# One table set for logarithm and exponential, an earlier query norm, and adaLN column sums by 32x32 transposes in a two-layer hybrid block

## The chip, the cores and the metric

The kernel runs on one core of one Trainium2 chip. The metric is the device time of one execution in microseconds (us). Engines are named as in the profile: PE (matrix multiply, with PEld for its weight loads), DVE (vector), ACT (scalar, with function tables), POOL, and the queue SP that issues most transfers.

## The reference, cut to what matters

Two layers over 256 tokens of width 1024, fp32. Each layer is: feed-forward, token mixer, feed-forward. Each of the three is preceded by an RMS norm that is modulated by columns of `mod` (adaLN), and its result is added through a gate column of `mod`.

```
cond = silu(c)                                   # one vector of 1024
for l in range(2):
    mod = cond @ w_ada[l] + b_ada[l]             # 1024 x 9216, split in 9
    h = rms_norm(x, g0) * (1 + sc1) + sh1
    x = x + 0.5 * g1 * swiglu(h, w_ff_in[l,0], w_ff_out[l,0])
    h = rms_norm(x, g1) * (1 + sc2) + sh2
    x = x + g2 * token_mix(h, ...)
    h = rms_norm(x, g2) * (1 + sc3) + sh3
    x = x + 0.5 * g3 * swiglu(h, w_ff_in[l,1], w_ff_out[l,1])
```

`token_mix` projects h to three branches. Branch a is windowed attention with RMS-normed queries and keys (logarithm and exponential for the norm, exponential for the softmax). Branch b is a gated linear recurrence with a short convolution (tanh, exponential, a square root made of logarithm and exponential, gelu). Branch c is chunked linear attention with decays (exponential, output norm). Sigmoid gates are made of tanh.

## The kernel before

Activations lie transposed: features on the 128 partitions, 256 tokens along the free dimension, x in eight chunks. Every fp32 weight matrix is read in slabs of 1024 x 256 (or 256 x 1024), 120 per layer. ACT rounds a slab to its high part (`hi`, L890), DVE subtracts to get the low part (`lo`, L1306), and PE makes each product in three passes (high-high, high-low, low-high; L460), 48 matmuls per slab. The four raw buffers, three high and three low buffers go round in turn, guarded by counters.

There are five programs written out by hand, one per engine, which meet only at semaphores. So the order on each engine is the order in the text. A wait is told below by its semaphore.

**Feed-forward.** `ff` runs j over 11 blocks of hidden features. In one step PE does the next gate slab, the down slab and the next up slab; ACT does silu and two or three `hi`; DVE does the product `t512b` (L1388), its low part (L1392), and three `lo`.

**adaLN.** `mod` is made in blocks of 512 columns, 18 per layer. For a block, DVE multiplies eight 128 x 512 pieces of `w_ada` by the entries of cond and sums them in `ada_acc` (`weigh`, L1225 and L1231, two halves per block). That leaves sums over 128 partitions still to be made. PE makes them in `ada(b)` (L504): four matmuls with a 128 x 128 piece of `ada_acc` as weights and a column of ones as the moving operand, so that each gives 128 sums down one PSUM column. DVE copies the four columns to `mod` (L1240). A table spreads the halves over steps j (`FF_HALVES`). In the feed-forwards, 20 blocks are made: six in each of the first three and two in the last. Six of the 20 are late: their `ada(b)` stands in the norm that follows, between the sum of squares (L554) and the first product. The 14 others stand in the steps j. Other blocks are made in the prologue (4) and beside the mixer's last products (12, four of them late, in the norm before the second feed-forward).

**Norm.** PE sums squares (L554). ACT makes rstd by logarithm (L897) and exponential (L899). DVE makes the modulation columns `ms` and `ma` (L1314 to L1317) from `mod`, then `hf` chunk by chunk (L1332); ACT rounds (L916), DVE subtracts (L1337), and PE starts its next product by chunks as they come (`by_chunks`, L485, or the key/value product, L605).

**Function tables.** ACT holds one set of functions at a time. Where the program asks for a function that isn't in the set that is loaded, the compiler puts an ACT_TABLE_LOAD in front of it. Before, the logarithm comes from one set and the exponential (with tanh) from another; gelu with tanh and silu with tanh come from two more; copy, square, identity and abs are in every set.

**Mixer, first part.** Four rounds i. Each has four slabs: queries (p), recurrence input (p+1), gelu gate (p+2), branch c gate (p+3). The softmax and the recurrence of round i-1 are done inside round i. In the order of each engine, round i has:

- PE: product p, product p+1, `turn_p(n-1)` (L633: twelve transposes of the probabilities into banks 4 to 7), the sum of the queries' squares (L678, bank 2), product p+2, the scores (L691, L692, into banks 4 to 7), the gates of the recurrence (L698), product p+3, `values(n-1)`.
- ACT: `hi(p+2)`, `exps(n-1)`, `decays(n-1)`, the queries' squares (L1052), `hi(p+3)`, the copy to `xcp` (L1058), two of the four transposed heads to SBUF (`turned_p`, L1010), in round 1 a logarithm (L1068), `root_ln`, the queries' rstd by `ln` (L962) and `ex` (L967), `root_ex`, `hi(p+4)`, gelu (L1084), tanh (L1091), `hi(p+5)`, tanh.
- DVE: `lo(p+2)`, `scale_p`, `lo(p+3)`, the convolution (L1485, L1489), the other two heads (`turned_p`, L1448), the scaled queries `qn` in `t512b` (L1501), `recur(n-1)` (L1454 to L1459, ends in `yb_ready`), `lo(p+4)`, the scores' bias (L1512) and maxima.

PE's scores wait for `qn_ready` and for both engines' `pT` copies; product p+3 waits for `gel_ready`, because gelu reads bank 3, and gelu waits for `yb_ready`.

**Mixer, second part.** Four rounds of branch c with `output_norm` (logarithm and exponential of two columns, L962 and L1130), followed by a tanh gate (L1116), then 16 gate and branch slabs beside which adaLN blocks are made.

Of the kernel before, what the change touches and what calls it, by code (L numbers as in the profile page):

```python
# [11 lines left out]
ALU = mybir.AluOpType  # L12
# [91 lines left out]
def build(nc, x, c, w_ada, b_ada, norm_g, w_ff_in, w_ff_out, w_in, qk_norm_g, attn_sinks, rel_bias,  # L104
# [3 lines left out]
    with ctx:  # L108
# [3 lines left out]
        def sem(name):  # L112
# [59 lines left out]
        ada_acc = scratch[:, 2048:4096].rearrange("p (u n) -> p u n", u=4)  # L172

# [3 lines left out]
        zw = sb("zw", [2 * T], BF16)  # L177
# [28 lines left out]
         consts_ready, c_loaded, small_loaded, x_loaded, c_turned, turned, x_turned, par_ready, lam_ready, lam_exp,  # L206
# [10 lines left out]
             "consts_ready c_loaded small_loaded x_loaded c_turned turned x_turned par_ready lam_ready lam_exp "  # L217
# [55 lines left out]
        def ff_closed(l, f, j):  # L273

            first, blocks = ff_ada(l, f)
            return [first + m for m in blocks_closed(FF_HALVES, j) if m < blocks]

# [171 lines left out]
        def _(pe):  # L449
# [21 lines left out]
            def zero(bank):  # L471
                mm(ps[:, bank, :], zw[:, 0:P], zw[:, :], start=True, stop=False, skip_group_check=True)
# [34 lines left out]
            def stay_busy(bank, times):  # L507

                for _ in range(times):
                    mm(ps[:, bank, :], zw[:, 0:P], zw[:, :], start=True, stop=True)  # L510


# [30 lines left out]
            for l in range(DEPTH):  # L543
                k0 = SLABS * l

                def norm(q):
# [9 lines left out]
                    for b in late(l, q):  # L556
                        ada(b)

                def ff(f, q):
# [18 lines left out]
                    for j in range(NF):  # L578
# [71 lines left out]
                for i in range(4):  # L650
# [182 lines left out]
        def _(act):  # L833
# [46 lines left out]
            for l in range(DEPTH):  # L880
# [19 lines left out]

                def squares(q):
# [83 lines left out]
                def exps(n):  # L985

                    act.wait_ge(max_ready, n + 1)
# [40 lines left out]
                for i in range(4):  # L1028
# [30 lines left out]
                    if i:  # L1059
                        turned_p(n - 1)  # L1060
                    if i == 0:
# [3 lines left out]
                        ln(krs, ps[:, 6, :], HD)  # L1065
                    if i == 1:
# [53 lines left out]
                def output_norm(n):  # L1120

                    act.wait_ge(o_done, n + 1)
# [72 lines left out]
        def _(dve):  # L1195
# [19 lines left out]
            def weigh(a):  # L1215
# [3 lines left out]
                if q == 0 and b >= 4:  # L1219
                    dve.wait_ge(ada_done, b - 1)  # L1220
# [13 lines left out]
                ins.then_inc(ada_weighed, 1)  # L1234

# [46 lines left out]

            lv = [lu[:, n, :].rearrange("p (l c) -> p l c", l=DEPTH) for n in range(6)]
# [13 lines left out]
            for l in range(DEPTH):  # L1297
# [21 lines left out]
                def norm(q):  # L1319
                    if l == 0 and q == 0:  # L1320
                        dve.wait_ge(par_ready, 2)
                    if l or q:
                        for b in late(l, q):
                            ada(b)
# [31 lines left out]
                def ff(e, q):  # L1356
# [6 lines left out]
                    for j in range(NF):  # L1363
# [34 lines left out]
                        if j > 0:  # L1398
                            for b in ff_closed(l, e, j - 1):
                                if b not in late_blocks:  # L1400
                                    ada(b)
                        for a in ff_halves(l, e, j):
                            weigh(a)
# [57 lines left out]
                for i in range(4):  # L1461
# [32 lines left out]
                    if i:  # L1494
                        turned_p(n - 1)
                    else:
# [5 lines left out]
                    if i:  # L1502
                        recur(n - 1)
# [193 lines left out]
```

## Time and profile before

| what | value |
|---|---|
| timed runs | 1638.91 us median of 3 (1638.63 to 1640.33) |
| the profiled execution, its own time | 1637.36 us |
| its span, first to last instruction | 1635.6 us |
| mean granted PE clock | 0.986 of full |
| table loads on ACT | 71 |

The profiled execution has 1.76 us outside its span. It lies 1.55 us under the median of the timed runs. Times inside a trace are us from the start of the span; a row's second number is how long its group of merged instructions took; `[1.48 <-DVE t512b L1501]` means that the engine was idle for 1.48 us before the row and that this instruction let it go.

### The profile page before, as it was taken

The page shows a single profiled execution, that of the slowest core. Times are in us where ns is not written, and L with a number is a line of the kernel's source. Part 1 is how long each engine was busy: PE and PEld are TensorE (multiplying, and loading weights), DVE is VectorE, ACT ScalarE, POOL GpSimd, SP SyncE. Part 2 cuts the span into 40 slices and gives each one's busy share as a digit, 9 for nine tenths or more (in the row PEclk, how much of TensorE's full clock was granted, in tenths as well). Part 3 has the DMA queues.
Part 4 walks back from the last instruction along what each step waited for, and adds up shares of the span by engine and source line. Part 5 has one row for each costly group of instructions (what it writes and reads, how often), then busy time and mean ns, then how long its engine had stood idle before and what let it go on. Part 6 is the DMA issues. An engine that isn't in the chain of part 4 may idle for free.

```text
span 1635.6 us, 29520 instructions
## 1 busy us (share of the span) xinstructions
PE 1590.2 (97%) x12797; PEld 1541.8 (94%) x12803; DVE 1077.7 (66%) x1400; ACT 813.4 (50%) x946; POOL 23.3 (1%) x27
## 2 busy tenths in 40 slices
PE   7999999999999999999999999999999999999998
PEld 6999998898999999999999999998899999999998
DVE  4676676787446986665666656659864578766454
ACT  3443335888445445333454334478855454453342
POOL 0000000000100000000000000000000100000000
PEclk8999999999999999999999999999999999999999
DMA  9789655554446885876747766444444489575551
GB/s 343 269 264 254 236 157 161 148 156 128 130 155 222 306 272 180 278 246 223 239 170 276 249 226 210 144 152 136 133 144 128 160 299 327 169 272 189 172 184 49
DMA packets 283744, 333.53 MB, mean 204 GB/s; under 512 B 13084, under 2 KB 234944, under 8 KB 283616
## 3 DMA queue, kind: packets, MB, share of 16 engines
q1 hardware_dynamic: 275856, 327.40, 60.8%
q10 hardware_dynamic: 7760, 4.26, 1.1%
q8 instruction: 101, 1.65, 0.4%
q14 instruction: 27, 0.22, 0.0%
HBM read 330.23 MB, written 1.38 MB: 203 GB/s over the span
## 4 chain that ended last, share of the span: by engine, by line
PE 83%; ACT 8%; DVE 6%; issue 2%; DMA 0%; SPq 0%; ACTq 0%; DVEq 0%
PE ps L460 69%; PE ps L769 3%; PE ps L485 2%; ACT w_hi L890 2%; PE ps L504 2%; DVE scratch L1489 1%; PE ps L503 1%; ACT pr L991 1%; ACT pr L989 1%; PE ps L605 1%; DVE scratch L1231 1%; ACT L989 1%; PE ps L698 1%; DVE hf L1332 1%; PE ps L734 1%
## 5 line engine op out<-in xcount | busy, mean ns | idle before, releaser
L460 PE MATMUL ps<-h_hi,w_hi 128*128 128x256 f32 x2464 | 704.5, 286 | 3.3 <-ACT scratch L1084 2.7
L460 PE MATMUL ps<-h_lo,w_hi 128*128 128x256 f32 x2464 | 697.3, 283 | 0.0
L460 PE MATMUL ps<-h_hi,w_lo 128*128 128x256 f32 x2464 | 697.2, 283 | 0.0
L1306 DVE TENSOR_TENSOR w_lo<-raw,w_hi 128x2048 fp32r<-128x2048 f32 x237 | 541.8, 2286 | 136.4 <-ACT w_hi L890 135.9
L890 ACT ACTIVATE w_hi<-raw 128x2048 fp32r<-128x2048 f32 x237 | 451.5, 1909 | 225.0 <-PE ps L460 219.5
L460 PEld LDWEIGHTS ps<-h_hi,w_hi 128*128 128x128 f32 x2464 | 472.8, 192 | 12.3 <-issue 6.7
L460 PEld LDWEIGHTS ps<-h_lo,w_hi 128*128 128x128 f32 x2464 | 473.0, 192 | 2.0 <-issue 1.9
L460 PEld LDWEIGHTS ps<-h_hi,w_lo 128*128 128x128 f32 x2464 | 472.9, 192 | 0.0
L460 PE MATMUL ps<-y_hi,w_hi 128*128 128x256 f32 x704 | 201.1, 286 | 0.0
L460 PE MATMUL ps<-y_lo,w_hi 128*128 128x256 f32 x704 | 199.1, 283 | 0.0
L460 PE MATMUL ps<-y_hi,w_lo 128*128 128x256 f32 x704 | 199.1, 283 | 0.0
L1231 DVE SCALAR_TENSOR_TENSOR scratch<-eyr,cond,scratch 128x512 f32<-128x512 f32 x240 | 180.3, 751 | 8.3
L1388 DVE TENSOR_TENSOR t512b<-t512a,ps 128x512 f32<-128x512 f32 x44 | 30.3, 688 | 197.8 <-issue 122.8
L460 PEld LDWEIGHTS ps<-y_lo,w_hi 128*128 128x128 f32 x704 | 135.0, 192 | 0.0
L460 PEld LDWEIGHTS ps<-y_hi,w_hi 128*128 128x128 f32 x704 | 135.0, 192 | 0.0
L460 PEld LDWEIGHTS ps<-y_hi,w_lo 128*128 128x128 f32 x704 | 135.0, 192 | 0.0
L460 PE MATMUL ps<-hid_hi,w_hi 128*128 128x256 f32 x384 | 109.0, 284 | 0.0
L460 PE MATMUL ps<-hid_lo,w_hi 128*128 128x256 f32 x384 | 108.7, 283 | 0.0
L460 PE MATMUL ps<-hid_hi,w_lo 128*128 128x256 f32 x384 | 108.7, 283 | 0.0
L932 ACT ACTIVATE t512a<-ps 128x512 f32<-128x512 f32 x44 | 26.3, 597 | 110.2 <-PE ps L460 100.3
L460 PEld LDWEIGHTS ps<-hid_lo,w_hi 128*128 128x128 f32 x384 | 73.7, 192 | 0.0
L460 PEld LDWEIGHTS ps<-hid_hi,w_hi 128*128 128x128 f32 x384 | 73.7, 192 | 0.0
(256 smaller groups left out, 1665.9 us busy)
## 6 DMA issues: line engine op xcount, KB each, us to landing
raw<-in_w_ff_in_dram SPq DMA_DIRECT2D x176, 512.0 KB, 4.8
eyr<-in_w_ada_dram SPq DMA_DIRECT2D x144, 512.0 KB, 6.9
raw<-in_w_in_dram SPq DMA_DIRECT2D x100, 512.0 KB, 4.7
raw<-in_w_ff_out_dram SPq DMA_DIRECT2D x88, 512.0 KB, 4.7
raw<-in_w_gate_dram SPq DMA_DIRECT2D x48, 512.0 KB, 4.6
raw<-in_w_branch_dram SPq DMA_DIRECT2D x48, 512.0 KB, 4.6
raw<-in_w_out_dram SPq DMA_DIRECT2D x16, 512.0 KB, 5.0
rgw<-in_rg_w_dram ACTq DMA_DIRECT2D x16, 128.0 KB, 2.8
```

What stands on the lines that cost most here:

```text
L460: last = mm(outs, a, b[:, cc, :], start=not rows and cc == 0 and q == 0, stop=cc == n - 1 and q == 2, skip_group_check=True)
L485: last = mm(ps[:, bank, t * T:(t + 1) * T], a, b[:, cc, :], start=False, stop=cc == C - 1 and q == 2, skip_group_check=True)
L503: mm(to, ada_raw(2 * b + 1)[:, cc, cols], cond[:, 4 + cc:5 + cc], start=cc == 0, stop=False)
L504: last = mm(to, acc[:, cols], ones[:, 0:1], start=not direct, stop=True)
L605: mm(ps[:, 4, 0:T], wkv[a][:, cc, 0:P], (h_hi, h_lo)[b][:, cc, :], start=cc == 0 and q == 0, stop=cc == C - 1 and q == 2, skip_group_check ...
L769: last = mm(ps[:, 1, m * T:(m + 1) * T], a, b, start=cc == 0 and q == 0, stop=cc == C - 1 and q == 2)
L890: f(w_hi[:, p % SPLIT, :], raw[:, p % RAW, :], ACT.Copy).then_inc(hi_ready, 1)
L932: f(t512a[:, :], ps[:, 4, :], ACT.Silu).then_inc(silu_ready, 1)
L989: f(pr[:, hh, 0:P], sc[:, hh, 0:P], ACT.Exp, bias=nmx[:, 0, hh:hh + 1], accum_out=sm[:, 0, hh:hh + 1])
L1231: ins = stt(acc, w[:, cc, :], by, acc, ALU.mult, ALU.add)
L1306: tt(w_lo[:, p % SPLIT, :], raw[:, p % RAW, :], w_hi[:, p % SPLIT, :].bitcast(F32), ALU.subtract).then_inc(lo_ready, 1)
L1388: tt(t512b[:, :], t512a[:, :], ps[:, 5, :], ALU.mult).then_inc(hid_made, 1)
```

## The change

It has four parts.

1. `ln_exp()` loads a set that holds both logarithm and exponential (but no tanh). It stands at the head of `norm`, `exps` and `output_norm`, ahead of their waits. After `root_ex` in the mixer's first part, gelu's set is loaded by name, ahead of `hi(p+4)`.
2. In the mixer's first part the sum of the queries' squares goes ahead of `turn_p` on PE, the queries' `ln`/`ex` ahead of `turned_p` and of both roots on ACT, and `qn` ahead of `turned_p` on DVE.
3. In the feed-forwards, when a block's second half is weighed, DVE transposes the 32x32 squares of the 128 x 512 sums, and sums each run of 32 by a row reduction to 16 columns of `ada_part`. When four blocks are there (and then the other two), PE does one matmul with a constant matrix `fold` as weights and 64 (or 32) moving columns, and DVE copies the result to `mod` by four copies of 32 partitions. The first group stands at j = 8 (PE) and 9 (DVE), the second in the norm that follows. The four late blocks from beside the mixer keep the old way.
4. The zero operand `zw` is half as wide and read twice by a broadcast.

```
+        fold = sb("fold", [P])
+            def ada_group(l, f, g):
+                first, blocks = ff_groups(l, f)[g]
+                s = first - ff_ada(l, f)[0]
+                pe.wait_ge(fold_ready, 4)
+                pe.wait_ge(ada_folded, folded_before(first + blocks))
+                pe.wait_ge(ada_saved, first)
+                mm(ps[:, 7, 0:16 * blocks], fold[:, :], ada_part[:, s:s + blocks, :].rearrange("p b n -> p (b n)"),
+                   start=True, stop=True).then_inc(ada_done, blocks)
...
-                    for b in late(l, q):
-                        ada(b)
+                    if q == 2:
+                        for b in late(l, q):
+                            ada(b)
+                    else:
+                        ada_group(l if q else l - 1, 1 - q, 1)
...
-                        if j > 0:
-                            for b in ff_closed(l, f, j - 1):
-                                if b not in late_blocks:
-                                    ada(b)
+                        if j == 8:
+                            ada_group(l, f, 0)
...
-                    else:
-                        turn_p(n - 1)
                     pe.wait_ge(qsq_ready, n + 1)
                     mm(ps[:, 2, :], halves[:, :], t512a[:, :], start=True, stop=True).then_inc(qss_done, 1)
+                    if i:
+                        turn_p(n - 1)
...
+                def ln_exp():
+                    act.preload_act_table_set("natural_log_exp_and_others")
...
                 def norm(q):
+                    ln_exp()
                     act.wait_ge(ss_done, 3 * l + q + 1)
...
                 def exps(n):
+                    ln_exp()
                     act.wait_ge(max_ready, n + 1)
...
-                    if i:
-                        turned_p(n - 1)
                     if i == 0:
...
                         ln(krs, ps[:, 6, :], HD)
+                        ex(krs, krs_ready)
+                    act.wait_ge(qss_done, n + 1)
+                    ln(rstd[:, :], ps[:, 2, :], HD)
+                    ex(rstd[:, :], qrs_ready)
+                    if i:
+                        turned_p(n - 1)
...
                     if i:
                         root_ln(n - 1)
-                    act.wait_ge(qss_done, n + 1)
-                    ln(rstd[:, :], ps[:, 2, :], HD)
-                    if i == 0:
-                        ex(krs, krs_ready)
-                    ex(rstd[:, :], qrs_ready)
-                    if i:
                         root_ex(n - 1)
+                    act.preload_act_table_set("gelu_apprx_tanh_and_others")
                     hi(p + 4)
...
                 def output_norm(n):
+                    ln_exp()
                     act.wait_ge(o_done, n + 1)
...
+            def fold_block(a, first):
+                b = a // 2
+                dve.wait_ge(ada_weighed, ada_before(a + 1))
+                steps.did(nc.vector.transpose(ada_turned, ada_acc[:, b % 2, :]))
+                if b == first:
+                    dve.wait_ge(ada_done, first)
+                steps.wait()
+                nc.vector.tensor_reduce(ada_part[:, b - first, :], ada_turned.rearrange("p (n k) -> p n k", k=32), AX.X,
+                                        ALU.add).then_inc(ada_folded, 1)
+            def ada_columns(l, f, g):
+                first, blocks = ff_groups(l, f)[g]
+                dve.wait_ge(ada_done, first + blocks)
+                columns = mod[:, :, :].rearrange("p l n -> p (l n)")
+                for q in range(4):
+                    rows = slice(32 * q, 32 * q + 32)
+                    last = cp(columns[rows, 4 * first:4 * first + 4 * blocks],
+                              ps[rows, 7, 0:16 * blocks].rearrange("p (n q) -> p n q", q=4)[:, :, q])
+                last.then_inc(ada_saved, blocks)
...
+                        if j == 9:
+                            ada_columns(l, e, 0)
                         for a in ff_halves(l, e, j):
-                            weigh(a)
+                            weigh(a, ff_ada(l, e)[0])
+                            if a % 2:
+                                fold_block(a, ff_ada(l, e)[0])
...
-                    if i:
-                        turned_p(n - 1)
-                    else:
+                    if i == 0:
                         dve.wait_ge(krs_ready, l + 1)
...
                     stt(t512b[:, :], ps[:, 0, :], par[:, l, B_QG:B_QG + 1], rstd[:, :], ALU.mult, ALU.mult).then_inc(qn_ready, 1)
                     if i:
+                        turned_p(n - 1)
                         recur(n - 1)
```

## Rows read from the trace of the kernel before

**Rows 1.** The page, busy time of each engine.
```profile
PE 1590.2 (97%) x12797; PEld 1541.8 (94%) x12803; DVE 1077.7 (66%) x1400; ACT 813.4 (50%) x946; POOL 23.3 (1%) x27
```

**Rows 2.** Waits of PE: us in total, times, longest.
```profile
PE ps L691 <- DVE t512b L1501: 9.8, 6, 2.3
...
PE ps L605 <- DVE h_lo L1337: 5.1, 2, 2.5
PE ps L485 <- DVE h_lo L1337: 4.4, 3, 1.5
...
PE ps L460 <- ACT scratch L1084: 2.7, 4, 1.1
```

**Rows 3.** Groups of instructions, ACT: the largest group of table loads.
```profile
L962 ACT ACT_TABLE_LOAD x10 | 12.8, 1283 | 0.2
```

**Rows 4.** Timeline of DVE, second feed-forward: start, us, engine, line, operation.
```profile
703.66 0.69 DVE L1388 TENSOR_TENSOR t512b<-t512a,ps 128x512 f32<-128x512 f32 x1 [3.33 <-issue]
...
721.82 0.69 DVE L1388 TENSOR_TENSOR t512b<-t512a,ps 128x512 f32<-128x512 f32 x1 [6.55 <-issue]
...
739.10 0.69 DVE L1388 TENSOR_TENSOR t512b<-t512a,ps 128x512 f32<-128x512 f32 x1 [6.36 <-issue]
...
745.60 0.16 DVE L1240 COPY mod<-ps 128x4 f32<-128x4 f32 x1 [0.80 <-PE ps L504]
...
828.73 0.88 DVE L1352 SCALAR_TENSOR_TENSOR xT<-ps,gcol,xT 128x256 f32<-128x256 f32 x2 [1.83 <-PE ps L460]
```

**Rows 5.** Groups of instructions, DVE: a reduction and a scan.
```profile
L1457 DVE TENSOR_TENSOR_SCAN scratch<-scratch 128x256 f32<-128x256 f32 x16 | 10.2, 679 | 0.3
...
L1520 DVE TENSOR_REDUCE mx<-scratch 128x4 f32<-128x512 f32 x8 | 5.4, 681 | 0.0
```

**Rows 6.** Timelines of ACT and DVE, norm ahead of the first mixer.
```profile
245.46 1.28 ACT L899 ACT_TABLE_LOAD   x1
246.75 0.42 ACT L899 ACTIVATE rstd<-rstd 128x256 f32<-128x256 f32 x1
...
247.12 0.17 DVE L1317 SCALAR_TENSOR_TENSOR ma<-ma,par 128x8 f32<-128x8 f32 x1
247.32 1.27 DVE L1332 SCALAR_TENSOR_TENSOR hf<-xT,ma,rstd 128x256 f32<-128x256 f32 x3
```

**Rows 7.** Norm ahead of the second feed-forward: timeline of DVE, then the chain.
```profile
633.29 0.17 DVE L1317 SCALAR_TENSOR_TENSOR ma<-ma,par 128x8 f32<-128x8 f32 x1
634.64 1.28 DVE L1332 SCALAR_TENSOR_TENSOR hf<-xT,ma,rstd 128x256 f32<-128x256 f32 x3 [1.18 <-ACT rstd L899]
...
636.46 8.62 PE ps L485 x48
```

**Rows 8.** Mixer's first part, rounds 1 and 3: timelines of DVE and PE.
```profile
311.34 1.02 DVE L1448 COPY scratch<-ps 128x384 f32<-128x384 f32 x2
...
315.18 0.69 DVE L1459 TENSOR_TENSOR eyr<-scratch 128x512 f32<-128x512 f32 x1
...
313.39 0.50 PE L691 MATMUL ps<-kk,t512b 64*128 64x128 f32 x4 [1.48 <-DVE t512b L1501]
...
317.89 0.39 PE L460 MATMUL ps<-h_hi,w_hi 128*128 128x256 f32 x1 [1.14 <-ACT scratch L1084]
...
369.92 1.12 PE L678 MATMUL ps<-t512a,halves 128*128 128x512 f32 x2 [0.36 <-ACT t512a L1052]
...
379.12 0.50 PE L691 MATMUL ps<-kk,t512b 64*128 64x128 f32 x4 [2.33 <-DVE t512b L1501]
```

**Rows 9.** PE after that wait: two us by windows (busy, clock, DMA), and the gates' matmuls.
```profile
380.00:382.00 2.00, 2.00 (x12) 0.50 0.00 0
...
314.76 1.99 PE L698 MATMUL ps<-scratch,rgw 128*128 128x256 f32 x8
...
1177.99 3.51 PE L698 MATMUL ps<-scratch,rgw 128*128 128x256 f32 x8
```

**Rows 10.** Timeline of PE, first adaLN block beside the mixer's last products.
```profile
531.30 1.02 PE L504 MATMUL ps<-ones,scratch 128*128 128x1 f32 x8 [0.82 <-DVE scratch L1231]
```

More of the change, by code:

```diff
@@ L172, in build @@
         ada_acc = scratch[:, 2048:4096].rearrange("p (u n) -> p u n", u=4)
+        ada_turned = scratch[:, 3072:3584]
+        ada_part = scratch[:, 3584:3680].rearrange("p (b n) -> p b n", b=6)
+        quarter = scratch[:, 1536:1568]
+        fold = sb("fold", [P])
         bias = sb("bias", [HEADS, 192])
@@ L176, in build @@
         dup = sb("dup", [2, 2, CH])
-        zw = sb("zw", [2 * T], BF16)
+        zw = sb("zw", [T], BF16)
         eps, tiny = sb("eps", [1]), sb("tiny", [1])
@@ L276, in ff_closed, with ff_groups, folded_before @@
             return [first + m for m in blocks_closed(FF_HALVES, j) if m < blocks]
+        def ff_groups(l, f):
+            first, blocks = ff_ada(l, f)
+            return [(first, min(blocks, 4))] + ([(first + 4, blocks - 4)] if blocks > 4 else [])
+        def folded_before(b):
+            return sum(max(0, min(b - first, blocks)) for first, blocks in (ff_ada(l, f) for l in range(DEPTH) for f in range(2)))
         def pair_halves(l, n):
@@ L471, in zero @@
             def zero(bank):
-                mm(ps[:, bank, :], zw[:, 0:P], zw[:, :], start=True, stop=False, skip_group_check=True)
+                mm(ps[:, bank, :], zw[:, 0:P], zw[:, :].unsqueeze(1).broadcast_to((P, 2, T)), start=True, stop=False,
+                   skip_group_check=True)
             def by_chunks(p, bank, moving, pieces_ready, before, per):
@@ L509, in stay_busy @@
                 for _ in range(times):
-                    mm(ps[:, bank, :], zw[:, 0:P], zw[:, :], start=True, stop=True)
+                    mm(ps[:, bank, :], zw[:, 0:P], zw[:, :].unsqueeze(1).broadcast_to((P, 2, T)), start=True, stop=True)
+            def ada_group(l, f, g):
[6 more added lines that the diff above has]
+                   start=True, stop=True).then_inc(ada_done, blocks)
             pe.wait_ge(consts_ready, 3)
@@ L1213, in _, with weigh @@
                     steps.did(cp(dup[:, g, r, :], ident[:, g * 64:(g + 1) * 64]))
-            def weigh(a):
+            def weigh(a, stage=None):
                 b, q = a // 2, a % 2
@@ L1219, in weigh @@
                 if q == 0 and b >= 4:
[L1220 removed]
+                    dve.wait_ge(ada_done, b - 1 if stage is None else stage)
                 acc, w = ada_acc[:, b if b < 4 else b % 2, :], ada_raw(a)
@@ L1281, in lam_product @@
                 steps.did(ts(hcn[:, :], lu[:, 5, :], 4.0, None, ALU.mult))
+            steps.did(nc.vector.tensor_reduce(quarter, ident[:, :].rearrange("p (b r) -> p r b", r=32), AX.X, ALU.add))
+            steps.wait()
+            for q in range(4):
+                cp(fold[:, 32 * q:32 * q + 32], quarter).then_inc(fold_ready, 1)
             lv = [lu[:, n, :].rearrange("p (l c) -> p l c", l=DEPTH) for n in range(6)]
@@ L1322, in norm @@
                     if l or q:
-                        for b in late(l, q):
-                            ada(b)
+                        if q == 2:
+                            for b in late(l, q):
+                                ada(b)
+                        else:
+                            ada_columns(l if q else l - 1, 1 - q, 1)
                     dve.wait_ge(ada_saved, ADA_BLOCKS * l + (4 + 6 * q))
@@ L1397, in ff @@
                             lo(down[j])
[L1398 to L1401, printed above, removed]
+                        if j == 9:
+                            ada_columns(l, e, 0)
                         for a in ff_halves(l, e, j):
-                            weigh(a)
+                            weigh(a, ff_ada(l, e)[0])
+                            if a % 2:
+                                fold_block(a, ff_ada(l, e)[0])
                     gate_column(2 if e == 0 else 8, 6 if e == 0 else 18)
```

4 lines of the change are left out of this document (2 added, 2 removed).

## Prediction

> **What bounds the kernel now.** The page first: PE is busy for 97% of the span, the others for 66% and less [rows 1]. So what can be won is PE's own instructions, and the 3% in which it stands still. For the second I read PE's waits [rows 2]: the scores behind `t512b`, the first products after a norm behind `h_lo`, product p+3 behind gelu. Nothing in the feed-forward steps waits. Then come the places: a feed-forward's steps [rows 4], two norms [rows 6, 7], the mixer's first part [rows 8], and what the clock does after a long wait [rows 9]. ACT's 71 loads take 1.283 us each [rows 3], 91 us, but only those ahead of which PE stands still count.
>
> **Feed-forward sums on PE.** A step with an `ada(b)` lasts 721.82 - 703.66 = 18.16 us, one without 739.10 - 721.82 = 17.28 [rows 4]. So a block costs PE 0.88, all of it on the path. 14 such blocks go: 12.3 us. In come four groups, each one matmul, two instructions where the block had eight. By count a group is 0.22; its 64 columns against one add something; a whole block, 0.88, is the bound above. I take 0.3, near the count: 1.2. Gain 11.1 (8.8 to 11.4). The second groups stand in norms, where PE waits anyway.
>
> What DVE pays: per block a transpose and a reduction of 512 elements. The reduction has a row, 0.68. For the transpose I have bounds: 0.68 as the reduction, and 1.36, twice the scan of 256, the slowest row per element [rows 5]. I take 0.68, since it too reads 512 elements once; 1.4 per block. It also loses the wait of 0.80 and the copy of 0.16 for each block [rows 4]. DVE idles 3.33 to 6.55 ahead of `t512b` in the steps [rows 4], so even 2.1 is covered. What is queued behind the fold is `lo` of the next gate slab, and behind that SP's reload of its raw buffer; both are two products (11 us) ahead of need. At the end of a feed-forward the last fold stands ahead of the gate column and the residual, where DVE has 1.83 left [rows 4]: 0.4 stays. Priced 0. Were the cover gone, the residual of the first chunks would slip first, and these come at PE's pace, slower than DVE's 0.8, so up to 1.5 more is caught up by the fourth. The constant `fold` is made while DVE waits for the first weights: 0.
>
> **Norms.** Five have both loads. In the norm ahead of the mixer the second load stands between logarithm and exponential (245.46 to 246.75), and `hf` starts at 247.32, while the modulation is done at 247.29 [rows 6]. So both paths must shorten. rstd comes 1.29 sooner. The modulation loses two blocks (1.76) and gets a group (0.3) and three more copies of small size (0.3): 1.16 sooner. Gain 1.1 in each of two such norms. In the norm ahead of the second feed-forward the two blocks stay; `ma` is done at 633.46 and `hf` waits until 634.64 [rows 7]: 1.15 before the modulation binds. Two such norms. In the first norm of layer 2 the group replaces the blocks, so only rstd binds: 1.28. Together 5.8. Early loading itself gives nothing there: the first load already runs ahead of a single wait.
>
> A page would price this differently. The Trainium skill (ScalarE: Activation LUTs, What ACT_TABLE_LOAD costs) says that a switch takes 1283 ns for the load and 1380 ns of drain, 2.66 us. The trace has the load but no drain: the exponential starts 1.29 after the load does [rows 6]. By the page the norms would give up to 4 more; the sum goes by the rows.
>
> **Mixer, first part.** ACT has two loads fewer in each of rounds 1 to 3, but both stand behind `hi(p+3)`, and the scores' wait goes through DVE: `lo(p+3)`, convolution, copies, `qn`. Round 1: the convolution ends at 311.34; `qn` then takes 0.66, the two copies 0.93 behind it, and the scores, which need both, go at 313.1 instead of 313.39 [rows 8]. That is what the moved copies cost: no more than 0.3 is won there. But the recurrence ends at 315.8 as before [rows 8], and gelu then needs no load: it is done by 316.4, when the gates' matmuls end too (313.1 + 3.36). Product p+3 goes at 316.5 instead of 317.89: 1.4. Round 2: the same wait is 0.2 (four such waits make 2.7 [rows 2]): 0.2. Round 0 is bound by DVE's sums, unchanged: 0.
>
> Round 3 is where the new order costs. `qsq_ready` comes late, behind four exponentials of 1024; before, the transposes lay in that hole and PE waited 0.36 [rows 8]. Now PE waits for 1.8 ahead of them: product p+2 is 1.4 late, and so is everything behind it on PE. But the scores wait 2.33 for DVE [rows 8], so the delay goes into that wait, and they still start at 379.1. What changes is the clock. After the wait of 2.33 the granted clock is 0.50 of 2.4 GHz, the 1.2 GHz level, and the gates' matmuls take 3.51 where round 1 has 1.99 [rows 9]. After 1.48 and 1.14 within 5 us it stayed up [rows 8, 9]. Split into 1.8 and 1.4, eight us apart, I expect it to stay up: 1.5. If it falls in the first hole, its cost goes into the slack: 0 lost. Per layer 3.1 (1.4 to 3.4), 6.2 in all.
>
> **Second part and last products.** `output_norm` loses one load, its tanh gate gains one (no tanh in the new set): PE waits for neither. Behind the last one `hi` comes 1.2 sooner, and through DVE's `weigh` that ends a wait of PE of 0.82 [rows 10]: 1.6 for two layers.
>
> **The clock after norms.** In the norm ahead of the second feed-forward PE's first 48 matmuls take 8.62 [rows 7], part of it at 1.2 GHz. With pieces 0.79 apart they would take 6.3. With `rstd` sooner the two holes there (0.93 and 1.48) become one of 1.4, short enough by the mixer's rows. Two norms could give 2.3 and 1.1. I take 2.0 of 3.4; bounds 0 and 3.4. In the other three the hole grows to 3, and nothing comes.
>
> **Sum.** 11.1 + 5.8 + 6.2 + 1.6 + 2.0 = 26.7. The profiled execution took 1637.4 (span 1635.6 and 1.8 around it), which gives 1610.7. It lies 1.55 under the median of the timed runs, so for those 1612.
>
> **Rivals.** First, DVE's order binds the mixer more than I see, so that its rounds give nothing: for it speaks that `qn` to the scores is DVE's chain and the two copies stand in it; against it that gelu's own load stood on the path with 1.14 behind it [rows 8]. 1618.
>
> Second, the holes after the norms cost more clock: each is as long as before or longer and falls at another moment. Then the norms give 1 instead of 5.8 and the clock nothing, with a mixer at half: 1624. For it: all holes of 2.3 and more ended in the low clock.
>
> Third, the fold is slow. It is hidden up to about 4 us per block; at 5, PE would wait 1 us in each of 14 steps, and the residuals late: 1626. Against: the slowest row gives 2.1.
>
> Fourth, more clock than I take, in the norms above all: 1604. The skill's drain would also end near there.
>
> On the other side: the loaded set isn't used. If the compiler still puts the first set with a logarithm ahead of each logarithm, and another ahead of the exponential, the loads asked for by name come on top: 71 become over 90. Then `exps` starts 1.28 later in six rounds and its roots bring two more loads ahead of the recurrence, about 2 each, 12; the norms lose about 1 each, 5; with 11 won on PE, some 6 slower: 1645. It decides as soon as a load stands between logarithm and exponential. Against it: tanh after an exponential has no load today, so a set is kept while it serves. The same rival covers that the change doesn't do what it says.
>
> **Chances.** Forecast (1606 to 1617) 0.66; DVE's order 0.13; holes 0.07; slow fold 0.02; more clock 0.07; set unused 0.05. About 0.2%, 3.3 us, is what can be told from no change. Everything but the last is faster by more: 0.95; of the last, 0.01 falls within, 0.04 slower. The range 1605 to 1621 takes the forecast, the first rival and part of the fourth; the unknown prices (group 2.3, mixer 3.4, clock 2) reach from 1608 to 1620.
>
> **What would show it.** 48 loads where 71 were, none between L962 and L967 or between logarithm and exponential of a norm. All steps of a feed-forward 17.3 apart, one with 0.3 more. `hf` 1.1 to 1.3 sooner after the sum of squares. Round 1: scores 0.3, product p+3 1.4 sooner; round 3: a wait of 1.8 ahead of the queries' sum and no low clock at the gates. A transpose of 0.7 on DVE. I'd be wrong if the low clock comes in round 3 anyway, if PE gets a wait for DVE in the steps, or if a load stands ahead of both.

## The result, and the profile after

The changed kernel takes 1611.74 us (median of four runs, 1607.62 to 1616.01); the kernel before, timed beside it, 1639.54. The ratio is 0.9831, interval 0.9805 to 0.9857: 27.8 us faster. The forecast was 1612.0, in a range of 1605 to 1621. The profiled execution took 1611.73, with a span of 1610.0; the prediction's sum on that basis was 1610.7. One execution of the kernel before, beside the later experiments, took 7268 us and is left out of the ratios.

The page, busy time by engine, against [rows 1]: PE lost 20 us of work, DVE has 29 more, ACT 28 less.

```profile
PE 1570.2 (98%) x12657; PEld 1521.6 (95%) x12657; DVE 1106.7 (69%) x1453; ACT 785.6 (49%) x923; POOL 23.3 (1%) x27
```

Groups of instructions: ACT's table loads, against [rows 3], and DVE's new work.

```profile
L928 ACT ACT_TABLE_LOAD x21 | 26.9, 1283 | 0.4
L1146 ACT ACT_TABLE_LOAD x10 | 12.8, 1283 | 0.2
L1107 ACT ACT_TABLE_LOAD x8 | 10.3, 1283 | 0.1
L962 ACT ACT_TABLE_LOAD x5 | 6.4, 1283 | 0.1
...
L1271 DVE STREAM_TRANSPOSE scratch<-scratch 128x512 f32<-128x512 f32 x20 | 14.2, 711 | 0.7
L1275 DVE TENSOR_REDUCE scratch<-scratch 128x16 f32<-128x512 f32 x20 | 13.7, 686 | 1.0
```

With four single loads these are 48, where 71 were. 21 are the new set's, asked for by name (L928), and none stands between a logarithm and an exponential behind the start (two of the single loads, at L894 and L896, belong to the norm in the start, which part 1 leaves alone): the rival of the unused set is out.

Waits of PE, against [rows 2]:

```profile
PE ps L630 <- DVE h_lo L1398: 6.1, 2, 3.1
PE ps L499 <- DVE h_lo L1398: 4.3, 3, 1.5
PE ps L716 <- DVE scratch L1509: 3.9, 4, 1.0
PE ps L701 <- ACT t512a L1083: 3.3, 2, 1.7
...
PE ps L716 <- DVE t512b L1560: 2.2, 2, 1.1
PE ps L473 <- DVE w_lo L1364: 1.7, 3, 0.6
```

The reader is to see three things. The wait of product p+3 for gelu, 2.7 before, has no row left. The scores (L716) wait 6.1 in all where it was 9.8, and four of the six times for the moved copies (L1509), as forecast for round 1. And the queries' sum (L701) waits 3.3 in its two third rounds, where it was 0.36 each.

DVE in the second feed-forward, against [rows 4], timeline (start, us):

```profile
690.04 0.71 DVE L1271 STREAM_TRANSPOSE scratch<-scratch 128x512 f32<-128x512 f32 x1
690.79 0.69 DVE L1275 TENSOR_REDUCE scratch<-scratch 128x16 f32<-128x512 f32 x1
695.62 0.69 DVE L1449 TENSOR_TENSOR t512b<-t512a,ps 128x512 f32<-128x512 f32 x1 [1.95 <-issue]
...
712.90 0.69 DVE L1449 TENSOR_TENSOR t512b<-t512a,ps 128x512 f32<-128x512 f32 x1 [6.62 <-issue]
...
730.18 0.69 DVE L1449 TENSOR_TENSOR t512b<-t512a,ps 128x512 f32<-128x512 f32 x1 [4.90 <-issue]
```

These steps are 17.28 us now, those with a block's fold too; steps of 18.16 are gone. DVE still idles ahead of `t512b`, but down to 1.95. One step in each feed-forward is longer, the one with the group's matmul:

```profile
782.02 0.69 DVE L1449 TENSOR_TENSOR t512b<-t512a,ps 128x512 f32<-128x512 f32 x1 [6.63 <-issue]
799.52 0.69 DVE L1449 TENSOR_TENSOR t512b<-t512a,ps 128x512 f32<-128x512 f32 x1 [1.52 <-PE ps L473]
```

That is 17.50, so a group costs 0.22.

Norm ahead of the first mixer, against [rows 6], ACT and then DVE:

```profile
243.60 1.28 ACT L928 ACT_TABLE_LOAD   x1
245.29 0.47 ACT L922 ACTIVATE rstd<-ps,eps 128x256 f32<-128x256 f32 x1 [0.41 <-PE ps L578]
245.80 0.42 ACT L924 ACTIVATE rstd<-rstd 128x256 f32<-128x256 f32 x1
...
245.44 0.69 DVE L1285 COPY mod<-ps 32x8 f32<-32x8 f32 x4 [0.32 <-PE ps L534]
...
246.44 0.17 DVE L1375 SCALAR_TENSOR_TENSOR ma<-ma,par 128x8 f32<-128x8 f32 x1
246.64 1.27 DVE L1393 SCALAR_TENSOR_TENSOR hf<-xT,ma,rstd 128x256 f32<-128x256 f32 x3
```

The exponential follows the logarithm at once. rstd is there at 246.2, the modulation at 246.6, and `hf` follows the modulation without a wait: the modulation binds here, as forecast.

The mixer's first part, against [rows 8]: PE in rounds 1 and 3.

```profile
313.10 0.50 PE L716 MATMUL ps<-kk,t512b 64*128 64x128 f32 x4 [0.98 <-DVE scratch L1509]
...
316.37 0.39 PE L473 MATMUL ps<-h_hi,w_hi 128*128 128x256 f32 x1
...
367.93 1.12 PE L701 MATMUL ps<-t512a,halves 128*128 128x512 f32 x2 [1.66 <-ACT t512a L1083]
...
377.09 0.50 PE L716 MATMUL ps<-kk,t512b 64*128 64x128 f32 x4 [0.99 <-DVE scratch L1509]
378.46 1.99 PE L723 MATMUL ps<-scratch,rgw 128*128 128x256 f32 x8
```

In round 1 the scores start at 313.10 (forecast 313.1) and product p+3 at 316.37 without a wait (forecast 316.5); the times can be compared as they stand, since product p+3 of round 0 starts at 286.37 before and at 286.36 after. In round 3 the one wait of 2.33 has become two, 1.66 (forecast 1.8) and 0.99, and the gates' matmuls take 1.99: they ran at 2.4 GHz. The 3.51 of [rows 9] is the second layer's; in this round of the first layer the kernel before has

```profile
381.25 2.84 PE L698 MATMUL ps<-scratch,rgw 128*128 128x256 f32 x8
```

To see where the rest went I cut the profiled executions at fixed instructions: the start of the last matmul of a norm's sum of squares, the start of the first product of a slab whose input is complete, the product p+3 of each round. The table gives the us between such starts. Feed-forward 1 counts from its first matmul of all; elsewhere the matmuls that go chunk by chunk behind a norm count to the norm. "First part" is the four rounds and the stretch up to the second part's first product.

```
stage                                      before   after
up to the first product of ff 1             46.49   50.13
ff 1, with its sum of squares              198.06  194.74
ff 2, likewise                             191.11  187.88
ff 3, likewise                             191.11  187.78
ff 4, to its last slab's products          185.97  184.51
norm ahead of mixer 1                       15.50   15.17
norm ahead of mixer 2                       16.45   14.43
norm ahead of ff 2                          14.19   11.46
norm ahead of ff 3                          13.95   11.79
norm ahead of ff 4                          13.06   11.46
first part, mixer 1: rounds 0 to 3, rest   139.52  136.07
first part, mixer 2                        139.60  136.06
second part, each                          231.15  230.11
end                                          8.26    8.27
```

Feed-forwards 11.3, norms 8.8, first parts 7.0, second parts 2.1: 29.3 gained, and 3.6 lost in the start, which the change hardly touches. Windows show what differs there; the column behind the four engines' and POOL's busy times is the granted clock. After:

```profile
24.00:34.00 10.00, 10.00 (x43) 8.25 (x42) 5.91 (x8) 3.03 (x3) 0.00 (x0) 0.66 1.05 378
34.00:44.00 10.00, 10.00 (x48) 8.12 (x48) 3.35 (x6) 5.74 (x8) 0.00 (x0) 0.59 1.08 371
44.00:50.00 6.00, 6.00 (x29) 3.02 (x27) 2.26 (x9) 1.17 (x3) 0.00 (x0) 0.83 1.00 367
```

and before:

```profile
24.00:34.00 10.00, 10.00 (x42) 8.25 (x42) 5.85 (x8) 3.28 (x3) 0.00 (x0) 0.66 1.06 377
34.00:44.00 10.00, 9.76 (x63) 7.03 (x64) 3.26 (x7) 5.37 (x8) 0.00 (x0) 0.83 1.08 371
44.00:47.00 3.00, 3.00 (x17) 1.57 (x16) 2.83 (x10) 1.53 (x4) 0.00 (x0) 1.00 1.07 389
```

PE is busy almost throughout, but after the change it spends some 17 us of the start at 1.2 GHz where it was 10. Whether the change does that was a question for the experiments.

### The profile page after: what moved, and what is told of

Read it like the earlier page. It is cut to its first block, busy times and chain, and to the rows that moved or that the text cites. A ratio compares the mean times of both kernels' runs of the same rounds, so it can differ in the third digit from the quotient of the medians.

```text
span 1610.0 us, 29256 instructions
## 1 busy us (share of the span) xinstructions
PE 1570.2 (98%) x12657; PEld 1521.6 (95%) x12657; DVE 1106.7 (69%) x1453; ACT 785.6 (49%) x923; POOL 23.3 (1%) x27
## 4 chain that ended last, share of the span: by engine, by line
PE 89%; DVE 5%; ACT 4%; issue 1%; DMA 0%; SPq 0%; ACTq 0%; DVEq 0%
PE ps L473 74%; PE ps L794 3%; PE ps L499 1%; ACT w_hi L915 1%; PE ps L517 1%; DVE scratch L1550 1%; PE ps L723 1%; PE ps L518 1%; PE ps L578 1%; DVE hf L1393 1%; PE ps L630 1%; DVE w_lo L1364 1%; DVE h_lo L1398 1%; ACT pr L1022 1%; ACT pr L1020 1%
```

## The experiments

Eleven experiments ran: ten kernels, and the changed one again. Each ratio is to runs of the kernel before on the same chip.

**The parts by themselves.** Four kernels take the diff apart; their edits are its hunks: `e1_sums` has the hunks of `fold`, `ada_group`, `fold_block` and `ada_columns`, and the narrower `zw` of part 4; `e2_sets` those of `ln_exp()` and of the load of gelu's set; `e3_order` the moved `turn_p`, `turned_p` and the queries' `ln` and `ex`; `e4_sets_order` the last two together.

> The kernel before with part 3 alone (feed-forward sums by transposes, row sums and one constant matmul). My theory: 14 blocks of 0.88 us leave PE's path and 4 groups of 0.3 come in, so each of the first three feed-forwards gives 3.2 us and the last 1.5, 11 in all; in the norms the logarithm's and exponential's loads still bind, so they give 0.1 or nothing. Ratio near 0.993. DVE's extra 1.4 us per block shows in no wait of PE. Rival (the sums shorten the norms too): 13 to 14 us. Rival (what is built for the constant matrix at the start delays the first product): the first feed-forward starts about 3.5 us later than in the kernel before, as it did in the profile of the changed kernel, and the gain is 7.5; my theory is that the start differs by the clock that a run happens to get, and not by this part.

Measured: 1627.4 us (1625.83 to 1627.77), ratio 0.9930 (0.9915 to 0.9945), as the theory said. But the profile has two things that it didn't: the first product starts at 50.66, 4.2 later than in the kernel before, and the norms take 2.2 less. Up to the first matmul behind it each norm takes what it took before, to 0.05 us, so the two loads still bind; the 2.2 is clock. The rival on the start has its late start here, though not its gain of 7.5, and falls by two later kernels, which hold the same `fold` and start at 46.74 (`e5_no_order`) and 46.81 (`e7_fill`).

> The kernel before with part 1 alone (one set for logarithm and exponential, gelu's set loaded ahead of hi(p+4)), the old order. 48 loads on ACT. My theory: three norms give 1.15 each until the modulation binds, the two ahead of the mixers give nothing (modulation at 247.29 binds); in the mixer's round 1 gelu's load leaves the path (1.3 us), round 2 gives 0.2, round 3 nothing with the wait of 2.3 and the low clock as before; the last wait beside the gates goes (0.8 a layer). 8 us (6 to 12), ratio 0.995. Rival (loads are hidden anyway): under 2 us.

Measured: 1627.32 us (1626.73 to 1634.85), ratio 0.9942 (0.9925 to 0.9959): 11.7 faster, at the upper end of the theory's 6 to 12. 48 loads; the three norms ahead of feed-forwards give 1.15 each up to the first matmul behind them and those ahead of the mixers nothing, as said.

> The kernel before with part 2 alone (queries' squares ahead of the transposes, queries' rstd ahead of the copies and roots, qn ahead of the copies), separate sets. Each round 1 to 3 then has two table loads more, because logarithm and exponential alternate twice: 83 loads. My theory: root_ex comes late, the recurrence and gelu with it, and rounds 1 and 2 lose 2 us each, round 3 about 1: slower by 8 to 10 us, ratio 1.005. So the new order pays only with the common set. Rival (the order itself is the gain, the sets are not): faster by 3 or more.

Measured: 1665.58 us (1661.47 to 1667.31), ratio 1.0161 (1.0146 to 1.0177): 26.6 slower, where 8 to 10 were expected. It has 87 loads, not 83, and the six rounds lose 22.1 us in its profile.

> The kernel before with parts 1 and 2, without the new sums. My theory: as the sets alone, and in round 3 a wait of 1.8 ahead of the queries' squares in place of part of the 2.3 ahead of the scores, no low clock there, 1.5 a layer more; 12 us (9 to 16), ratio 0.9925. The three parts then add up: sums 11 + this 12 is near the 25.6 of the profiled change. Rival (the sums are needed for the mixer's gain): the mixer's rounds give less here than in the changed kernel, by 2 us or more per layer.

Measured: 1626.28 us (1621.45 to 1627.98), ratio 0.9920 (0.9902 to 0.9938), near the expected 12. Its rounds take 30.02, 30.34 and 33.64, as those of the changed kernel: the mixer's gain doesn't need the sums.

By stages, the sums alone give the feed-forwards 3.3, 3.3, 3.3 and 1.55 (198.06, 191.11, 191.11, 185.97 become 194.74, 187.78, 187.78, 184.42), 11.5 in all, and nothing in the mixers' rounds. The set alone gives 1.5 and 0.57 in rounds 1 and 2, 1.04 in each second part, 6.7 at the norms (some of it clock), and in round 3 1.3 in one layer and nothing in the other. `e1_sums` and `e2_sets` both started late, at 50.66 and 50.13 us, `e4_sets_order` at 46.37: the start's clock belongs to no part of the change, and the totals of the first two must be read without it. Set aside, the set alone gives some 14 us, set and order 15.8.

What `e3_order` does is in ACT's timeline of round 1 and in PE's waits:

```profile
311.82 1.28 ACT L962 ACT_TABLE_LOAD   x1
313.82 1.28 ACT L967 ACT_TABLE_LOAD   x1
316.53 1.28 ACT L1072 ACT_TABLE_LOAD   x1
319.51 1.28 ACT L1020 ACT_TABLE_LOAD   x1
```

```profile
PE ps L460 <- ACT scratch L1082: 20.3, 6, 4.1
```

With the queries' root by itself, the logarithm and the exponential each load their table, and again for the recurrence's roots. All of it stands ahead of gelu, which product p+3 awaits: 20.3 us in six rounds where it was 2.7 in four [rows 2]. The reordering is only to be had with the common set.

**Is the reordering worth anything with it?** The changed kernel with the three moves undone:

```diff
                     pe.wait_ge(qsq_ready, n + 1)
                     mm(ps[:, 2, :], halves[:, :], t512a[:, :], start=True, stop=True).then_inc(qss_done, 1)
-                    if i:
-                        turn_p(n - 1)
```

(`turn_p` stands ahead of the wait again, `turned_p` and the roots likewise.)

> The changed kernel with the order of the mixers' rounds as it was before: the turn of the probabilities stands ahead of the sum of the queries' squares again, one table set for both functions and the new sums of the feed-forwards stay. My theory since the parts were run alone: with one set for both functions the rounds already take 30.0 and 30.3 us, so the reordering is worth only a stretch of low clock in round 3, at most 1.4 us a layer. It expects 1611 to 1614.5 us, with 30.0 and 30.3 us in rounds 1 and 2. Rival, from the sum of my prediction, which gave round 3 to the reordering in both layers as a wait that goes: 3 us over the changed kernel, 1615 us, with 35 us in both third rounds.

Measured: 1615.85 us (1614.82 to 1616.58), ratio 0.9858 (0.9841 to 0.9876). Rounds 1 and 2 took 30.02 and 30.34, as both said; the third rounds 36.20 and 35.03 where the changed kernel has 33.64. That is the rival's reading, mine of a smaller worth falls. PE in the third round:

```profile
373.55 0.81 PE L716 MATMUL ps<-kk,t512b 64*128 64x128 f32 x4 [2.34 <-DVE t512b L1564]
...
376.12 3.78 PE L723 MATMUL ps<-scratch,rgw 128*128 128x256 f32 x8
```

The wait is whole again, 2.34, and the gates' matmuls run at 1.2 GHz behind it. In `e2_sets`, with the same order and the same wait, they did so in one of the two third rounds (35.03, and 33.65 in the other). With the wait split in two, seven profiles (the changed kernel, twice, and `e4_sets_order`, `e6_turn4` to `e9_fill_start`) show it in none of 14 third rounds, all 33.64 or 33.65. With the single wait, the five profiles that have it (the kernel before, `e1_sums`, `e2_sets`, this one and `e11_before_fill`) show it in 8 of 10. Per pair of third rounds the reordering is worth 4.0 us here, 1.4 in `e2_sets`, and it was worth less than nothing without the common set.

**What DVE's fold costs.** The changed kernel with each transpose done four times:

```diff
+                for _ in range(3):
+                    steps.did(nc.vector.transpose(ada_turned, ada_acc[:, b % 2, :]))
+                    steps.wait()
                 steps.did(nc.vector.transpose(ada_turned, ada_acc[:, b % 2, :]))
```

> The changed kernel with each of the 20 blocks' 32x32 transposes done four times, so that VectorE carries 3 x 0.77 = 2.3 us more a block, 46 us in all. My theory: VectorE's part of the new sums is hidden wherever it stands, since VectorE idles some 5.3 of 20 us in the feed-forwards; no product waits for a block's sums. It expects the changed kernel's time within 2 us, 1610 to 1614 us, the feed-forwards at 194.7 and 187.8 us. Rival: VectorE's order binds in the chunks in which it is already busy 18.5 of 20 us, and the weights' low halves come late: each block that stands there costs up to 2.3 us, the time is 1620 to 1650 us.

Measured: 1617.45 us (1617.22 to 1619.16), ratio 0.9869 (0.9853 to 0.9884). Neither side had it: of 46 us more on DVE some 6 come through. The feed-forwards take 197.64, 188.93, 188.92 and 185.47, and PE has a wait that grew from 1.7 to

```profile
PE ps L473 <- DVE w_lo L1367: 5.2, 8, 1.0
```

What slips first is `lo` of the next slab, queued behind the fold, as the prediction named; but it slips at 3.5 us per block (four transposes and a reduction) already, so the "up to about 4" of the third rival was beyond the edge in the fullest steps. PE's waits cover about half of the 6 us. By steps, three in each feed-forward slip (17.56, 17.83 and 17.49 in the second and third, 1.0 in all); in the first feed-forward these take 17.56, 18.48 and 17.83, and the one with the group 19.10. At the fold's real 1.4 the feed-forwards run at PE's pace.

**The clock at the norms.** The changed kernel with products of zeros in PE's holes:

```diff
                         ada_group(l if q else l - 1, 1 - q, 1)
+                    stay_busy(5, 10 if q == 1 else 4)
...
                     pe.wait_ge(rstd_ready, 3 * l + q + 1)
+                    if l or q:
+                        stay_busy(5, 4)
```

> The changed kernel with products of zeros laid in TensorE's idle stretches at the five norms: ten ahead of the wait for the mixers' first product, four and four around the wait for the root ahead of the feed-forwards, 0.22 us each. My theory: after each idle stretch of 3 us TensorE runs 3.4 to 6.8 us at 1.2 GHz, which costs 1 to 2 us a time; three such stretches lie at the norms of the changed kernel (245.0, 828.7 and 1026.7 us), so filling them gives 2 to 5 us: 1607 to 1610 us, and the low stretches at the norms go. Rival: the low stretches don't follow from the idle time, or the fillers themselves come late: 1611 to 1615 us.

Measured: 1608.58 us (1606.99 to 1610.22), ratio 0.9812 (0.9797 to 0.9828). No stretch of low clock is left at any norm. (The three of the changed kernel begin at 247.4, 831.1 and 1029.0 us; the places in the expectation are some 2.4 us early.) Windows at the first mixer, without and with the fillers:

```profile
247.00:249.00 2.00, 0.55 (x2) 0.58 (x3) 2.00 (x6) 1.57 (x4) 0.00 (x0) 0.59 1.08 378
249.00:251.00 2.00, 2.00 (x10) 1.83 (x9) 2.00 (x6) 1.27 (x3) 0.00 (x0) 0.50 1.08 348
```

```profile
243.00:245.00 2.00, 1.23 (x6) 0.38 (x4) 1.93 (x7) 1.18 (x3) 0.00 (x0) 1.00 0.96 305
245.00:247.00 2.00, 1.59 (x9) 1.22 (x9) 2.00 (x6) 1.16 (x4) 0.00 (x0) 1.00 1.10 364
```

But the norms themselves win only 1.2 us by it (15.17 to 14.43, 11.79 to 11.32): at full clock PE then waits for pieces of DVE's `h_lo` (ten waits in the mixers' norms, 3.2 us). The rest of the profiled gain, 3.3, is the start at 46.81, which the edit doesn't touch. Theory right on the clock, too high on its worth.

**The start.** The changed kernel with `stay_busy(0, 14)` and `stay_busy(0, 8)` cut to 2 each:

> The changed kernel with 4 instead of 22 products of zeros ahead of the first feed-forward. The profile of the changed kernel shows TensorE without a gap from 13.8 us to its first product at 49.9 us, 17 us of it at 1.2 GHz, with 7.4 us spent on these products of zeros; before the change it started at 46.5. Theory: where the clock is low in the start, the products of zeros are the path, and without them the first product starts at 46 us or less whatever the clock: 1608 to 1611 us. Rival: a transfer or VectorE sets the start, and the products of zeros only kept the clock up: the first product starts at 46 to 50 us and then runs at 1.2 GHz for 3.4 us or more: 1611 to 1614 us.

Measured: 1607.84 us (1605.04 to 1609.86), ratio 0.9807 (0.9790 to 0.9824). The first product starts at 43.29. Those matmuls were on the path. The products that follow run at 1.2 GHz for 1.5 us, the first feed-forward takes 194.74 all the same, and 3.2 us stay, against even the earlier start of the kernel before. Behind it the norm ahead of the first mixer takes 1.0 more than in the changed kernel (16.19).

**Both, again, and the kernel before with the same.** `e9_fill_start` joins the last two edits, `e10_after_again` is the changed kernel unedited, `e11_before_fill` the kernel before with both edits.

> The changed kernel with both: products of zeros in TensorE's idle stretches at the norms, and 4 instead of 22 of them ahead of the first feed-forward. Theory: the two act in different places and add. Filled norms alone took 1608.6 us with the first product at 46.6 us; with the start at 42.9 us, as the shorter start alone had it, 3.7 us less: 1605 us (1603 to 1607), no stretch of 1.2 GHz behind the first feed-forward's start. Rival: the clock's low stretch only moves to the first feed-forward, and costs there what the start gained: 1607 to 1609 us.

Measured: 1606.83 us (1603.90 to 1607.85), ratio 0.9794 (0.9781 to 0.9808). The fastest of all, just inside the theory's range and just under the rival's. Whether the two add isn't shown: the profiled execution, the slowest of the five, has its first product at 46.38 us, with 1.2 GHz from 40.1 to 47.0, where the shorter start alone had 43.29. Two of the five took 1604, which is what adding would give.

> The changed kernel once more, unedited, beside the two with products of zeros on the same chip. If the spread of its first runs (1607.6 to 1616.0 us) is that of the start's and the norms' stretches of low clock, its profile shows these at other places or in another number, and the sum of the feed-forwards and rounds stays at what it was: median 1609 to 1614 us. If the fillers gain nothing, it comes within 1 us of the filled kernel.

Measured: 1613.92 us (1607.66 to 1616.15), ratio 0.9839 (0.9818 to 0.9860). Its profile repeats the first one's to 0.2 us in every stage, the start at 50.30 included, so it shows the low stretches at the same places and not at others. It is 7.1 us above the filled kernel. The single runs of both, sorted, are 1607.6, 1607.7, 1611.7, 1611.8, 1611.9, 1615.9, 1616.0, 1616.2: three levels, 4.2 us apart. No profile fell on the outer two, so where these 4.2 us lie stays open. One step may be the start: of the ten profiles with all 22 products of zeros ahead of the first product, four have the first product at 46.4 to 46.8 us and six at 50.1 to 51.0, and both profiles of the changed kernel are among the six. That the steps are stretches of low clock fits the records (granted clock 0.993, 0.990, 0.988 from fastest to slowest) and is not shown.

> The kernel before the change with the same products of zeros at the norms and the same shorter start. It measures what the change is worth where the norms' clock can't help it. My prediction's sum without its clock terms at the norms is 24.7 us; theory: this kernel takes 24 to 26 us more than the changed one with the same products of zeros, about 1630 us. Rival: much of the gain at the norms was clock, so the difference shrinks to 20 to 23 us, 1625 to 1628 us.

Measured: 1633.02 us (1629.78 to 1635.82), ratio 0.9962 (0.9949 to 0.9975). The difference to `e9_fill_start` is 26.2: just over the theory's 24 to 26, not the rival's 20 to 23. Between these two every norm runs at full clock but one, and the stages give what the change is worth there without the clock's help: 1.0, 1.1, 1.3 and 1.1 in four norms and 0.1 in the fifth, whose filled run fell to 1.2 GHz at 1026.6 us; feed-forwards 3.3, 3.3, 3.3, 1.5; first parts 3.3 and 3.5; second parts 1.0 each.

This kernel holds one more reading. In its first third round the gates' matmuls ran at 2.4 GHz behind the wait of 2.35, and yet the round took 34.84, as before (34.95 and 34.85, at 1.2 GHz). PE's waits in that stretch, `e11_before_fill`:

```profile
PE ps L694 <- DVE t512b L1504: 2.3, 1, 2.3
PE ps L460 <- ACT scratch L1087: 1.1, 1, 1.1
```

The second row is product p+3 waiting for gelu. With the gates at 2.4 GHz this wait stands open; at 1.2 GHz they fill it.

## Why the prediction was right

**Feed-forward sums**, forecast 11.1: measured 11.3 in the changed kernel, 11.5 alone. A block's 0.88 was right. A group costs 0.22 (a step of 17.50 against 17.28), the figure of the count; the 0.3 taken was a little high. The transpose, taken at 0.68 from the reduction's row, is 0.711.

**Norms**, forecast 5.8 and 2.0 more for the clock: measured 8.8. From the last matmul of the squares to PE's first matmul behind the norm, the five give 1.01, 1.01, 1.15, 1.15 and 1.28, 5.6 in all, against 1.1, 1.1, 1.15, 1.15 and 1.28. The filled pair gives 4.6, and 5.6 with the disturbed norm at the worth of its like, so rstd and modulation were priced right. The clock gave about 3, not 2, because the step "in the other three the hole grows to 3, and nothing comes" was wrong for two of them: the norms ahead of feed-forward 3 and mixer 2 won 2.2 and 2.0, against 1.28 and 1.1. At the mixer the hole did grow, from 2.5 to 3.1, and ahead of feed-forward 3 its first half from 0.93 to 1.21, but the low stretch behind it became shorter (3.4 us instead of 6.8 at both). At the first mixer, with the same hole of 3.1, it went the other way (6.8 instead of 3.4), and that norm won 0.3. So the size of the hole doesn't give the clock behind it, and part of the 3 us is luck. `e5_no_order`, `e6_turn4` and `e8_start` have the same norms: the one ahead of mixer 2 takes 15.29, 15.82 and 14.87 there, where the changed kernel's profile has 14.43. Only the gain ahead of feed-forward 3 comes in all of them (11.3 to 11.7).

**Mixer, first part**, forecast 3.1 a layer: measured 3.45 and 3.54. Round 1 gave 1.5 (1.4), round 3 1.3 and 1.2 (1.5). Round 2 gave 0.55 where I had 0.2: a term mis-sized, since I took what four waits for gelu left over as all there was to gain. In round 3 waits of 1.66 and 0.99 came where 1.8 and 1.4 were forecast. The size was near and the step was not: "What changes is the clock" is half of it. `e11_before_fill` has the clock up without the change and gains nothing, since PE then waits 1.1 for gelu and its load; `e5_no_order` has the load gone and loses the clock. The 1.3 needs both, gelu's load gone and the clock up. The common set gives the first, and the split wait gave the second in 14 of 14 rounds, where the single one left it to chance: in `e2_sets` one of the two third rounds had the whole 1.3 without it. The prediction also took 3.51 for the gates' matmuls in both layers; the first layer's took 2.84, and the two rounds still won the same, as they must if gelu bound them.

**Second parts**, forecast 0.8 each: 1.04.

**The clock at the start**, not in the sum: 3.6 lost in the profiled execution. It cancels what norms and rounds gave above their prices, which is why the total hit 1611.7 against 1610.7. The nearness is better than the terms deserve: 29.3 gained for 26.7 forecast, 3.6 lost for 0. Which of its two starts each profile caught is luck.

**Rivals.** DVE's order does bind the scores (its copies are the last releaser in four rounds), but gelu's missing load stood on the path all the same, as the prediction held against that rival. The holes after the norms: three grew, two shrank to one of 1.44 as forecast, and the clock gave 3 at the five together and took only at the first mixer; that rival is out. Slow fold: out at 711 ns. More clock, 1604: not by itself; the fastest of eight runs took 1607.6. A switch of tables costs its load and no more: at the norm ahead of ff 2 the logarithm starts at 627.83, 1.30 behind the load at 626.53. By the Trainium skill (ScalarE: Activation LUTs, What ACT_TABLE_LOAD costs) 1380 ns of drain come on top; the trace doesn't agree, here as in [rows 6].

## What to carry to other kernels

A table load is worth its 1.28 us only where an engine that sets the pace waits behind it; 23 loads went here, 30 us of ACT, and about 14 us of the time, clock at the norms included. A reordering and a shared table set can belong together so closely that one alone costs more (26.6 us) than both bring (12.7): test the parts singly before keeping either. And where the bounding engine has a wait such as the 2.3 us here, behind which the clock fell in 8 of 10 rounds, ask whether it can be split or filled before asking whether it can be shortened; the fillers on the path of the start, which has 10 us and more at low clock, cost more here than they kept.

## What the runs showed of the hardware

Low clock came in stretches of 3.4, 6.8 or 10.2 us in the traces' clock records, and a wait of 3.1 us in the same place of two norms left 6.8 us of it once and 3.4 the other time. The matmuls agree with the record to 0.2 us: at the norm ahead of ff 3 it has 1.2 GHz from 831.1 to 834.5. A window (granted clock 0.51) and PE's timeline of the changed kernel:

```profile
831.00:833.00 2.00, 2.00 (x12) 2.00 (x11) 2.00 (x7) 1.35 (x3) 0.00 (x0) 0.51 1.05 391
```

```profile
830.79 0.30 PE L499 MATMUL ps<-h_hi,w_hi 128*128 128x256 f32 x1
...
831.24 0.41 PE L499 MATMUL ps<-h_hi,w_hi 128*128 128x256 f32 x1
...
834.44 0.30 PE L499 MATMUL ps<-h_hi,w_hi 128*128 128x256 f32 x1
```

At the very start the granted clock isn't to be trusted. For 14 to 18 us of the kernel before the windows give 1.00, but its matmuls take what the same ones take in the low stretch from 24.6 us on (1.84), and not what they take at 2.4 GHz:

```profile
16.09 1.84 PE L503 MATMUL ps<-cond,eyr 128*128 128x1 f32 x8
...
22.48 1.03 PE L503 MATMUL ps<-cond,eyr 128*128 128x1 f32 x8
```

Later in the start PE fell to 1.2 GHz while the page has it busy almost without a gap; most of its matmuls there have one column. A transpose in 32x32 blocks of 128x512 takes VectorE 711 ns, within 4% of a reduction of as many elements.
